# First layer's merge: seven half products for the latent half of nine gate projections, modulation sums dealt between them in fours, and whole tiles around the first output norm

## The reference, cut to what matters

```python
def merge(p, ya, yb, yc):
    return (jax.nn.sigmoid(p[13]) * ya + jax.nn.sigmoid(p[14]) * yb
            + jax.nn.sigmoid(p[15]) * yc) @ w_out
...
def rms_norm(x, g):
    xf = x.astype(jnp.float32)
    y = xf * lax.rsqrt(jnp.mean(xf * xf, axis=-1, keepdims=True) + EPS)
...
o = rms_norm(o, norm_g).reshape(b_, t_, GLA_V).astype(gate.dtype)
return (o * jax.nn.silu(gate)) @ w_o
...
shift_x, scale_x, gate_x = jnp.split(jax.nn.silu(c) @ w_mod + b_mod, 3, axis=-1)
```

## Time and profile before

| | |
|---|---|
| time, median of 3 | 3189.71 us (3188.95 to 3189.86) |
| the profiled execution: its own time, its span | 3197.47 us, 3195.7 us |
| PE busy, share of the span | 3111.4 us, 97% |
| DVE, ACT, POOL busy | 1371.2, 847.9, 1546.8 us |
| mean granted clock of TensorE | 0.987 |
| HBM read, mean rate | 232.43 MB, 73 GB/s |

### The profile page before, as it was taken

One profiled execution on the slowest core, in us unless ns is written; L12 is line 12 of the kernel. 1 busy time (PEld: TensorE's weight loads), 2 busy tenths in 40 slices (PEclk: granted clock), 3 DMA queues, 4 the chain that ended last, 5 costly groups with the idle time before them and its releaser, 6 DMA issues.

```text
span 3195.7 us, 40388 instructions
## 1 busy us (share of the span) xinstructions
PE 3111.4 (97%) x15051; PEld 2275.2 (71%) x15051; DVE 1371.2 (43%) x2583; ACT 847.9 (27%) x1548; POOL 1546.8 (48%) x1451
## 2 busy tenths in 40 slices
PE   7998998999999999999999999999999999999999
PEld 3675675656666547566788768888995688889965
DVE  3022336545644422336676564444333364443332
ACT  4222225421111022424512122332111123322111
POOL 1689988100000029994264325787560157875610
PEclk9998999999999999999999999999999999999999
DMA  7111101014443221200234322222222222222212
GB/s 233 53 40 27 34 14 41 14 60 132 132 145 99 85 65 41 60 27 14 68 123 149 115 80 67 72 74 77 69 67 66 68 79 80 67 80 67 75 38 74
DMA packets 260204, 237.12 MB, mean 74 GB/s; under 512 B 20994, under 2 KB 257452, under 8 KB 260012
## 3 DMA queue, kind: packets, MB, share of 16 engines
q1 hardware_dynamic: 260012, 234.54, 24.1%
HBM read 232.43 MB, written 2.10 MB: 73 GB/s over the span
## 4 chain that ended last, share of the span: by engine, by line
PE 91%; DVE 6%; ACT 1%; issue 1%; SPq 1%; DMA 0%; DVEq 0%; ACTq 0%
PE ps L1256 26%; PE ps L496 25%; PE ps L541 12%; PE ps L1089 6%; PE ps L527 3%; PE ps L1318 2%; PE ps L819 2%; PE ps L956 1%; PE ps L1364 1%; DVE arena L1953 1%; PE ps L1195 1%; PE ps L832 1%; DVE arena L1949 1%; DVE small L2238 1%; PE ps L513 1%; PE ps L856 1%
## 5 line engine op out<-in xcount | busy, mean ns | idle before, releaser
L2680 POOL TENSOR_TENSOR arena<-arena,posi 128x512 f32<-128x512 f32 (+1 forms) x360 | 418.5, 1163 | 30.0
L541 PE MATMUL ps<-hT,wring 128*128 128x512 f32 (+1 forms) x1120 | 415.9, 524 | 11.0 <-ACT arena L1417 10.9
L541 PEld LDWEIGHTS ps<-hT,wring 128*128 128x128 f32 x1120 | 210.6, 193 | 173.0 <-issue 152.0
L496 PE MATMUL ps<-hT,wring 128*128 128x512 f32 (+1 forms) x960 | 324.9, 499 | 0.5 <-ACT arena L1417 0.5
L1417 ACT ACTIVATE arena<-ps 128x256 f32<-128x256 f32 (+4 forms) x395 | 171.7, 435 | 575.2 <-PE ps L496 206.7
L2763 POOL TENSOR_TENSOR arena<-wring 128x512 f32<-128x512 f32 x72 | 91.9, 1276 | 467.5 <-PE ps L1256 291.0
L496 PEld LDWEIGHTS ps<-hT,wring 128*128 128x128 f32 x960 | 184.4, 193 | 136.5 <-issue 124.5
L496 PE MATMUL ps<-arena,wring 128*128 128x512 f32 (+1 forms) x768 | 278.6, 522 | 0.0
L1949 DVE TENSOR_TENSOR arena<-arena 128x768 f32<-128x768 f32 (+6 forms) x122 | 170.4, 1397 | 235.6 <-ACT arena L1417 232.0
L2679 POOL TENSOR_SCALAR posi<-arena,cols 128x512 f32<-128x512 f32 (+1 forms) x360 | 250.7, 696 | 35.4
L1417 ACT ACTIVATE arena<-ps,cols 128x256 f32<-128x256 f32 (+2 forms) x172 | 100.8, 586 | 575.3 <-PE ps L541 242.9
(11 more groups left out here) (271 smaller groups left out, 5065.9 us busy)
## 6 DMA issues: line engine op xcount, KB each, us to landing
wring<-in_w_in SPq DMA_DIRECT2D x126, 1024.0 KB, 5.4
wring<-in_w_mod SPq DMA_DIRECT2D x24, 1024.0 KB, 8.7
wring<-in_w_out SPq DMA_DIRECT2D x24, 1024.0 KB, 5.6
wring<-in_w_ada SPq DMA_DIRECT2D x22, 1024.0 KB, 5.2
wring<-in_w_gla_out SPq DMA_DIRECT2D x7, 512.0 KB, 6.2
wring<-in_w_attn_out SPq DMA_DIRECT2D x7, 512.0 KB, 5.5
wring<-in_w_conv_out SPq DMA_DIRECT2D x6, 512.0 KB, 6.2
arena<-in_x SPq DMA_DIRECT2D x1, 2048.0 KB, 8.2
```

Of the source, the lines that this page charges most:

```text
L496: last = eng.matmul(o_(out), a, b_, start=(i == 0), stop=(i == len(parts) - 1))
L541: mm = eng.matmul(bank[b][:, 0:n], w[:, k, j * P:(j + 1) * P], hT[:, k, t0:t0 + n], start=(k == 0), stop=(k == KD - 1))
L2680: pool.link(eng.tensor_tensor(dst, dst, scratch, ALU.add))
```

## The change

Of the first layer's four quarters, three (`GATES7 = 3`) project the x half of their gates by seven half products: nine gates in all. The c half stays as it was. Each of these gates adds four POOL sums of weights, an ACT copy, three DVE combinations and one DVE corner sum, and an ACT sigmoid over the corner part. The last two of the seven products of a gate (`gate_corners`) run after the c tiles of the next gate, or, for the third gate, inside the first branch product. The weight slot of a gate is used up only then. `modulation_parts` of layer 0 stops after every four instructions, and DVE deals these parts between the combinations. Scratch for the sums are `posi`, `gscan`, `gup` and `rope`, so the last three are loaded again before layer 1. Around the first output norm PE now runs whole tiles (4 + 4 parts instead of 3 + 3), and ACT takes the first of them out before the norm's square roots. Layer 1's norm, with 2 + 2 parts before and after, is as it was.

```diff
+GATES7 = 3
...
+        h_sums0 = [rope[:, :, :].rearrange("p a b -> p (a b)").rearrange("p (a b) -> p a b", b=HALF)] + \
+            [mT[:, 4:8, i * HALF:(i + 1) * HALF] for i in range(3)]
+        g_t1 = posi[:, :].bitcast(F32).rearrange("p (a b) -> p a b", b=P)
+        g_t2 = gscan[:, 0:TX].rearrange("p (a b) -> p a b", b=P)
+        g_u2, g_w2 = gup[:, :], arena[:, A0 + A1 + A2 - HALF:A0 + A1 + A2]
...
             def gla_out_norm(l, p, between):
-                for _ in range(len(segs(l)) + 1):
+                for _ in range(2 * len(segs(l))):
                     next(between)
                 gla_square_sums(l, p)
-                for _ in range(len(segs(l)) + 1):
+                for _ in range(2 * len(segs(l))):
                     next(between)
                 gla_spread(l, p)
...
+                def gate_products(a, b_, w):
+                    g = ("gate", a, b_)
+                    x_, y_ = ((2, 3), (6, 7))[(3 * a + b_) % 2]
+                    left, right = bank[x_], bank[y_]
+                    for j in range(2):
+                        project(("mgate", 0, a, b_, j, "c"), w, j * P, hT, KD, "c")
+                    if b_:
+                        gate_corners(a, b_ - 1)
+                    claim(x_)
+                    seventh(left[:, 0:HALF], quarter[0][0], w[:, 0:4, 0:P], True)
+                    eng.wait_ge(*at(("m7 sums", g)))
+                    eng.wait_ge(*at(("h sums0",)))
+                    seventh(left[:, HALF:TX], h_sums0[1], g_t2).then_inc(*pe.tell(("m7 p16", g)))
+                    claim(y_)
+                    seventh(right[:, 0:HALF], h_sums0[2], w[:, 0:4, P:2 * P], True)
+                    seventh(right[:, HALF:TX], h_sums0[0], g_t1).then_inc(*pe.tell(("m7 p5", g)))
+                    bank_of["left", g], bank_of["right", g] = left, right
+                    last_on[x_], last_on[y_] = ("left", g), ("right", g)
+                    eng.wait_ge(*at(("m7 u2", g)))
+                    seventh(left[:, 0:HALF], quarter[0][1], w[:, 4:8, 0:P]).then_inc(*pe.tell(("full", ("left", g))))
...
+                def gate_corners(a, b_):
+                    g = ("gate", a, b_)
+                    w, right = gate_w[a, b_], bank_of["right", g]
+                    eng.wait_ge(*at(("m7 c22", g)))
+                    eng.wait_ge(*at(("m7 t4", g)))
+                    seventh(right[:, 0:HALF], quarter[1][1], w[:, 0:4, 0:P])
+                    seventh(right[:, HALF:TX], h_sums0[3], w[:, 4:8, P:2 * P]).then_inc(*pe.tell(("full", ("right", g))))
+                    plan[gate_plan[a, b_]][1] = ("full", ("right", g))
...
                         w = weights(wv(wi, C_M + b_ * D + a * 256, 256), KD, 256)
-                        for j in range(2):
-                            for sg in segs(l):
-                                project(("mgate", l, a, b_, j, sg), w, j * P, hT, KD, sg)
-                        used(("full", ("mgate", l, a, b_, 1, segs(l)[-1])))
+                        if a < GATES7:
+                            gate_w[a, b_], gate_plan[a, b_] = w, len(plan) - 1
+                            gate_slot[a, b_] = plan[-1][2], landed[plan[-1][2]]
+                            gate_products(a, b_, w)
+                        else:
+                            for j in range(2):
+                                for sg in segs(l):
+                                    project(("mgate", l, a, b_, j, sg), w, j * P, hT, KD, sg)
+                            used(("full", ("mgate", l, a, b_, 1, segs(l)[-1])))
...
                         for j in range(2):
                             for sg in segs(l):
                                 project(("mout", l, a, b_, j, sg), w, j * P, res[:, 4 * b_:4 * b_ + 4, :], 4, sg)
+                            if b_ == 0 and j == 0 and a < GATES7:
+                                gate_corners(a, 2)
...
+                if p or l == 0:
                     next(between, None)
...
+                    def gate_others(b_):
+                        v, b0 = gate_tile(b_)[0], B_M + 8 * b_ + 2 * a
+                        eng.wait_ge(*at(("free", ("right", ("gate", a, b_)))))
+                        fn(v[:, 0, TC + HALF:T], v[:, 0, TC + HALF:T], ACT.Sigmoid, bias=col(l, b0))
+                        fn(v[:, 1, TC:T], v[:, 1, TC:T], ACT.Sigmoid, ("gates", a, b_), bias=col(l, b0 + 1))
...
+                        if a < GATES7:
+                            if b_:
+                                gate_others(b_ - 1)
+                            g = ("gate", a, b_)
+                            eng.wait_ge(*at(("m7 p16", g)))
+                            fn(U1, bank_of["left", g][:, 0:HALF], ACT.Copy, ("m7 u1", g))
+                            evac(("left", g), mg[:, 2 * b_, TC:TC + HALF], 0, HALF, ACT.Sigmoid, bias=col(l, B_M + 8 * b_ + 2 * a))
...
                     for k in range(1, KD):
-                        if k == KD - 2:
+                        stt(sums, w[:, k, :], cT[:, col0 + 8 * c + k:col0 + 8 * c + k + 1], sums, M_, A_,
+                            ("mod summed", L, g) if (c, k) == (ncol - 1, KD - 1) else None)
+                        if (c, k) == (ncol - 1, KD - 1):
+                            done.append((L, g))
+                        if k in ends:
                             yield
                             dve.stage("modulation")
-                        stt(sums, w[:, k, :], cT[:, col0 + 8 * c + k:col0 + 8 * c + k + 1], sums, M_, A_,
-                            ("mod summed", L, g) if (c, k) == (ncol - 1, KD - 1) else None)
-                done.append((L, g))
...
                     for a in range(4):
+                        sums = chain(*[modulation_parts(L, g, (KD // 2 - 1, KD - 1)) for L, g in mod_groups(l, a)])
                         dve.stage("modulation")
-                        for L, g in mod_groups(l, a):
-                            modulate(L, g)
+                        def sum_parts(n):
+                            for _ in range(n):
+                                next(sums)
+                            dve.stage("merge")
+                        def gate_combined(b_):
+                            g = ("gate", a, b_)
+                            left, right = bank_of["left", g], bank_of["right", g]
+                            eng.wait_ge(*at(("m7 u1", g)))
+                            tt(g_u2, left[:, HALF:TX], U1, A_, ("m7 u2", g))
+                            eng.wait_ge(*at(("m7 p5", g)))
+                            tt(g_w2, right[:, 0:HALF], g_u2, A_)
+                            tt(gate_tile(b_)[0][:, 1, TC + HALF:T], right[:, HALF:TX], g_w2, A_, ("m7 c22", g))
+                        def gate_corner_sums(b_):
+                            g = ("gate", a, b_)
+                            eng.wait_ge(*at(("full", ("right", g))))
+                            tt(gate_tile(b_)[1], bank_of["right", g].rearrange("p (a b) -> p a b", b=HALF),
+                               g_u2.unsqueeze(1).broadcast_to([P, 2, HALF]), A_, ("free", ("right", g)))
+                        if a < GATES7:
+                            for b_ in range(3):
+                                sum_parts(2)
+                                if b_:
+                                    gate_corner_sums(b_ - 1)
+                                sum_parts(1)
+                                gate_combined(b_)
+                            sum_parts(2)
+                            gate_corner_sums(2)
+                        for _ in sums:
+                            pass
...
+                pool.stage("merge")
+                for sg in ("x", "c"):
+                    eng.wait_ge(*at(("free", ("csq", 0, sg))))
+                eng.wait_ge(*at(("branch", 0, 2)))
+                four_sums(quarter, h_sums0, ("h sums0",))
+                ahead = None
+                for a in range(GATES7):
+                    for b_ in range(3):
+                        g, (slot, count) = ("gate", a, b_), gate_slot[a, b_]
+                        w = slot_view(slot, KD, 256)
+                        eng.wait_ge(m.sem(f"w_slot{slot}"), count)
+                        if ahead:
+                            eng.wait_ge(*at(("m7 p5", ahead)))
+                        pool.link(eng.tensor_tensor(g_t1, w[:, 0:4, P:2 * P], w[:, 0:4, 0:P], ALU.subtract))
+                        pool.link(eng.tensor_tensor(g_t2, w[:, 4:8, P:2 * P], g_t1, ALU.subtract))
+                        eng.wait_ge(*at(("full", ("mgate", 0, a, b_, 1, "c"))))
+                        pool.link(eng.tensor_tensor(w[:, 0:4, P:2 * P], w[:, 4:8, P:2 * P], w[:, 0:4, P:2 * P], ALU.subtract),
+                                  ("m7 sums", g))
+                        eng.wait_ge(*at(("m7 p16", g)))
+                        pool.link(eng.tensor_tensor(w[:, 0:4, 0:P], w[:, 4:8, 0:P], g_t2, ALU.subtract), ("m7 t4", g))
+                        ahead = g
+                pool.stage("conv")
...
                 if l:
-                    eng.wait_ge(*at(("full", ("z", (l - 1, 1, 1), "c"))))
```

(3 more changed lines are left out.)

46 lines of the change are left out of this document (31 added, 15 removed).

## The result

The changed kernel took 3202.97 us (median of 9 runs) and the kernel before 3190.28 us (9 runs): ratio 1.0037, 95% interval 1.0026 to 1.0048. On a second chip it was 1.0024 (1.0015 to 1.0034). The forecast was 3190 us with a range to 3199; the time lies outside. Two executions of later kernels stood far off all others and are in no median: 9853.66 us with the wait filled by 11 calls, and 5173.7 us with one input, so that this kernel was profiled again.

What follows compares the result with a forecast made beforehand. PE, busy 97% of the span, was taken to bound the kernel. Merge +13.1, norm -13.6 and attention +1.0 summed to +0.5 us on the median of 3189.71, so 3190 us, range 3182 to 3199.

Steps and rivals of the forecast that it cites:

- The gates: First layer's merge: a changed gate takes 19.0 us on PE against 20.64, nine times, -14.8 us.
- The wait that takes its place: Merge: PE waits 5.0 us for DVE's group 3 sums, once in each changed quarter, +15.0 us.
- The first gate: Quarter 0: PE waits 2.7 us for POOL's third sum and 1.8 for DVE's first combination, +4.5 us.
- The clock behind the waits: Merge: half speed costs 2.4 us behind each 5 us wait, 7.2 for three, plus 1.2 at the first gate.
- The norm: First output norm: neither bank is waited for any more; with 1.7 us charged for the clock, -13.6 us.
- The attention: Some 15 us more of attention lie beside POOL's convolution: +0.6 us, taken as +1.0 (0 to 2).
- The reloads and the late weights: Reloading `gscan`, `gup` and `rope` is hidden by w_out products, nothing charged; merge weight loads fit by 2.4 and 0.2 us.
- the rival of late weights: Merge: gate slots free later, so weights come late; six places wait 1.5 us each, 9 us, giving 3199; chance 0.28.
- the clock holds: Merge: 5 us of waiting don't bring the clock down, 8.4 us stay away, giving 3182; chance 0.22.

Runs made afterwards that it cites:

- the wait filled by 11 calls: Changed kernel with 11 matmul calls, their product used by nobody, in PE's wait for group 3: 3194.59 us against 3192.16, ratio 1.0004.
- one input: Changed kernel with attention's one-column scalings given one tensor input and a per-partition scalar: 3189.00 us, ratio 0.9989; repeated 3189.13 us, ratio 0.9982.
- Group 3 early: Changed kernel with DVE dealing three more parts of sums ahead of the third gate's corner sum: 3180.96 us against 3190.38, ratio 0.9970.
- the kernel with the norm alone: Kernel before with only the norm edits on PE and ACT: 3182.71 us, ratio 0.9967.
- both repairs: Changed kernel with three more sum parts ahead of the third gate's corner sum and DVE's very first gate combination ahead of its sums: 3176.68 us, ratio 0.9958.

## Why the prediction was wrong

**The gates: right.** Predicted -14.8. A quarter without the wait is 93.3 instead of 98.0 us: -4.75 each, -14.3. Quarter 3, which I gave nothing, is 0.6 us shorter.

**The wait that takes its place: right.** Predicted 5.0 us, three times; measured 5.06, in every profile, at the place named and for the reason given: DVE idle ahead of the corner sum with the work undone. Group 3 early removes it.

**The first gate: right in sum.** Predicted 4.5 and 1.2 for the clock, 5.7 together. POOL's third sum took 4.05 us and PE waited 2.52 (2.7 predicted). DVE's combination cost 3.63 or nothing (1.8 predicted): that the mean of both comes out near is luck. Quarter 0 is 107.7 us on average; without the wait of 5.06 and the 2.9 us of clock behind it, it is 6.4 us over the 93.3 of the others.

**The clock behind the waits: mis-sized, the first step that failed.** I took 2.4 us each, at most 3.1; it is 3.4 (2.4 to 3.9), so 10.1 and not 7.2. The mean lay between bounds taken from a wait of 2.1 us and one of 7.3. The upper bound was half of the 6.2 us that the lower level outlasted the longer wait; behind the waits of 5.06 us it lasted up to 7.8 us. Merge: -14.3 - 0.6 + 15.2 + 10.1 + 6.4 = +16.8; the four profiles give 410.5 - 393.5 = +17.0, against +13.1 forecast.

**The norm: right.** Predicted -13.6. With the edits it is 66.7 us in all four profiles; without them 80.3 and 78.5, and 80.0 and 80.1 in two kernels that left it alone: -13.0 on average. The drop of the clock that I charged behind the one-column sums is there, once.

**The attention: the second step that failed.** I had 15 us more of it run beside POOL, costed by PE's busy share in two windows at +0.6, taken as +1.0 with an upper bound of 2. The share was read at 540 to 560 us, where POOL's instructions had 256 columns. The part that moved came to lie beside those of 512, which last 1.27 us instead of 0.73, and a scaling of DVE that falls into one mostly ends with it. Four profiles of the changed kernel average 253.6 us; three without the norm edits (249.7, 251.0, 250.0) average 250.2: +3.4, and single profiles up to 6.1 above the first of these. It depends on how the two lists fall together: the kernel with the norm alone, whose attention was moved about as far, took 250.5 us.

**The reloads and the late weights.** PE never waits for a weight or a table in the merge of the changed kernel, and the stretch behind it (1052 to 1100 us of the kernel before) takes 48.1 us in both. Nothing was due, as forecast; the rival of late weights fell.

**The sum.** +17.0 - 13.0 + 3.4 = +7.4 us, close to the second chip (+7.7). Of the difference of 6.9 us to the forecast 2.9 are the clock, 2.4 the attention, 0.7 the first gate, 0.6 the norm. The traced sum would give 3197 us, still inside the range: the two steps explain why the forecast was too low, but not why the first comparison ends beyond 3199. A change under 0.2% was also less hidden than I wrote: with nine runs each the interval is 0.11% to either side. The rival "the clock holds" was refuted at all three places.

**What stays open.** The first comparison gives +12.7 us, 5 more than the traces; part of that may be noise, as its interval (8.3 to 15.3 us) overlaps that of the second chip (4.8 to 10.9). The changed kernel's four profiled executions (3194.8 to 3200.8) all lie below both medians of its runs (3201.4 and 3203.0), and so does that of group 3 early (3171.4 against 3181), though not that of both repairs (3181.4 against 3176.7). The changed kernel's slower runs have a lower granted clock (0.981 to 0.984 where the fastest have 0.986, in the first comparison), so they spend more time at the lower level. Where they spend it no profile showed.

## What to carry to other kernels

When work moves along another engine's list, compare what instructions stand on the other side at the new time, form by form; a busy share from the neighbourhood doesn't tell it. A producer that idles in front of an order-fixed step with later work undone is the place to mend a wait: deal that work ahead of the step, rather than moving the consumer. And a wait on PE costs more than its length: 5.06 us cost 8.7 in quarters 1 and 2.

## What the hardware did that was not expected

- A DVE instruction over a single column with two inputs from SBUF took 0.16 us alone and up to 1.23 beside a POOL addition of 1.28 us; the same with one input and a per-partition scalar 0.21 us everywhere. In the kernel before that edit alone is worth 0.21%.
- Matmuls whose result nobody reads, placed in a wait of PE, took some 3.6 us off quarters 1 and 2 by keeping the clock at 2.4 GHz: better only than waiting, since removing the wait gave 8.7.
- Far from any edit, stretches that are alike in every kernel differed by steps of 3.3 us from execution to execution: behind the 4-column matmuls near 2600 us the clock sometimes fell and sometimes not (603.7 against 600.3 us).
